# Decode key scores moved into the projection stage, and expert rows added to the residual by indirect DMA, in a hybrid decoder layer on one Trainium2 core

## What is computed

```python
h = rmsnorm(x)
sq, sk, sv, dq, dk, dv, ga, gb = split(h @ w_in)          # 3*512, 3*768, 2*1024 columns
# branch A, stick-breaking attention, 8 heads of 64, for prompt rows over the prompt,
# for the 8 decode rows over 16 pages of 128 keys each, found through page_table:
z = q @ k.T / 8 + bias
a = exp(log_sigmoid(z) + sum of log_sigmoid(-z) over the later keys);  oA = a @ v
# branch B, dilated windows (128,1), (512,4), (2048,16), joined by their denominators -> oB
x = x + (sigmoid(ga) * (oA @ w_br_a) + sigmoid(gb) * (oB @ w_br_b)) @ w_out
# experts: 8 of 64 per token, weights w, plus one shared expert
h2 = rmsnorm(x)
x = x + shared(h2) + sum over the token's 8 experts of w * (silu(h2 @ wg[e]) * (h2 @ wu[e])) @ wd[e]
```

## Time and profile before

| | us |
|---|---|
| median of 3 runs | 2694.28 (2693.86 to 2694.97) |
| profiled execution | 2692.04 |
| its span, first to last instruction | 2690.2 |
| mean granted TensorE clock | 0.919 |
| busy: PE, DVE, ACT, POOL | 2252.5, 1063.6, 649.8, 685.6 |

### The profile page before, as it was taken

The page is one execution under the profiler, slowest core; times in us unless marked ns, Lnnn a source line. Parts: engine busy times, 40 slices in busy tenths (PEclk is TensorE's granted clock), DMA queues, the critical chain, the costliest instruction groups (busy, mean ns, idle before and its releaser), DMA issues. The chain is left out here.

```text
span 2690.2 us, 35840 instructions
## 1 busy us (share of the span) xinstructions
PE 2252.5 (84%) x12724; PEld 1687.6 (63%) x12724; DVE 1063.6 (40%) x1742; ACT 649.8 (24%) x1136; POOL 685.6 (25%) x711
## 2 busy tenths in 40 slices
PE   7999996492787869999799765999999999999910
PEld 6778674481343336666454524888998888889800
DVE  3000786555999720000022521333333333333367
ACT  5322221261443420000011001232232223222300
POOL 2121331000454420000000173222222222222166
PEclk9999998695899989999899887999999999999955
DMA  6657334324777750188231245999998998989788
GB/s 202 227 169 245 133 113 160 118 87 151 218 239 237 236 194 20 31 353 342 90 117 57 68 111 199 323 321 326 323 324 314 328 317 324 326 323 326 283 331 317
DMA packets 195136, 600.13 MB, mean 223 GB/s; under 512 B 27006, under 2 KB 71503, under 8 KB 168536
## 3 DMA queue, kind: packets, MB, share of 16 engines
q1 hardware_dynamic: 139200, 462.79, 49.6%
q0 software_dynamic: 24448, 77.12, 8.1%
q10 hardware_dynamic: 31392, 59.01, 5.9%
HBM read 475.54 MB, written 167.28 MB: 239 GB/s over the span
## 5 line engine op out<-in xcount | busy, mean ns | idle before, releaser
L1996 PE MATMUL pG_e<-xT,w_e 128*128 128x160 f32 x4224 | 627.0, 302 | 2.3 <-issue 1.3
L1996 PEld LDWEIGHTS pG_e<-xT,w_e 128*128 128x128 f32 x4224 | 586.4, 197 | 29.4 <-issue 26.5
L2102 DVE TENSOR_TENSOR w_e_lo<-w_e,w_e_hi 128x2048 fp32r<-128x2048 f32 x66 | 151.3, 2292 | 323.9 <-ACT w_e_hi L2043 323.9
L1379 PE MATMUL pG<-turned,w_gates 128*128 128x344 f32 x768 | 227.7, 455 | 20.3 <-DMA w_gates<-in_w_in 20.3
L504 PE MATMUL pP<-wring,hT_hi 128*128 128x512 f32 (+2 forms) x576 | 226.9, 394 | 4.9 <-POOL wring L307 3.9
L2043 ACT ACTIVATE w_e_hi<-w_e 128x2048 fp32r<-128x2048 f32 x66 | 126.1, 1911 | 399.0 <-DMA w_e<-in_w_e_down 385.1
L505 PE MATMUL pP<-wring,hT_hi 128*128 128x512 f32 (+2 forms) x576 | 221.3, 384 | 0.0
L506 PE MATMUL pP<-wring,hT_lo 128*128 128x512 f32 (+2 forms) x576 | 221.3, 384 | 0.0
L1379 PEld LDWEIGHTS pG<-turned,w_gates 128*128 128x128 f32 x768 | 147.1, 192 | 96.7 <-issue 21.6
L2092 DVE COPY xT<-pX 128x512 f32<-128x512 f32 x132 | 90.7, 687 | 246.2 <-PE pX L1980 246.2
L1958 POOL COPY index<-slot_token 128x1 int32 (+1 forms) x66 | 39.4, 597 | 576.3 <-PE pX L1983 570.0
(11 more groups left out here) (251 smaller groups left out, 3396.1 us busy)
## 6 DMA issues: line engine op xcount, KB each, us to landing
w_e<-in_w_e_gate SPq DMA_DIRECT2D x66, 1024.0 KB, 8.8
w_e<-in_w_e_up SPq DMA_DIRECT2D x66, 1024.0 KB, 11.4
w_e<-in_w_e_down SPq DMA_DIRECT2D x66, 1024.0 KB, 6.4
y_scratch<-zero SPq DMA_DIRECT2D x5, 8704.0 KB, 56.2
y_scratch<-y_e ACTq DMA_DIRECT2D x66, 512.0 KB
turned<-in_cache_sb_kv SPq DMA_DIRECT2D x128, 256.0 KB, 3.1
vbuf<-in_cache_sb_kv SPq DMA_DIRECT2D x128, 256.0 KB, 3.1
out<-in_cache_win_kv SPq DMA_DIRECT2D x8, 4094.0 KB, 18.7
```

Source lines behind the costliest of these rows:

```text
L1379: last = pe.matmul(pG[:, i % 2, k, :NC], wg[:, f // 2 % 2, k, c, (f % 2) * P:(f % 2 + 1) * P], hT[:, c, cols], start=(c == 0), stop=(c == ...
L1996: last = pe.matmul(pG[:, k, f * BLK:(f + 1) * BLK], wv[:, c, f, :], xT[:, r, c, :], start=(c == 0), stop=(c == KC - 1))
L2102: dve.tensor_tensor(wlo[:, r, :], w[:, r, 2, :], whi[:, r, :].bitcast(F32), ALU.subtract).then_inc(wlo_ready, 1)
```

## The change

1. Keys of the decode rows. Their loads, products and reductions leave the stick-breaking stage and are put into the projection: SP starts chunk n (of 32) after the store of item n + 9, VectorE scores it in its turn n + 10. There are two key buffers instead of four, in rows of `turned` that are free then; the scores go to DRAM (`sz`, 0.5 MB) and come back at the start of stick-breaking. There each decode row's remaining steps begin one tick into its five ticks instead of five, and values are loaded without waiting for keys.
2. Expert rows. `y_scratch`, its zeros and the combining stage are gone. The table of slots also carries the pair's weight, ScalarE's copies multiply by it, and GpSimd adds the rows into x2 with two indirect transfers per block, four blocks behind its gathers. Unused slots name spare rows 1032 to 1191 of h2 and x2, which are zeroed in the output stage. A last stage copies x2 to the outputs.

Projection:

```diff
+                def load_keys(n):
+                    s, c = divmod(n, NPC)
+                    if n >= NKB:
+                        sp.wait_ge(s_prod_ready, n - NKB + 1)
+                    if c == 0:
+                        sp.dma_start(q[:, s % 2, :], sc["samp"][s:s + 1, 0:SBW].broadcast_to([P, SBW])).then_inc(q_in[s % 2], 16)
+                    for j in range(GP):
+                        pg = sp.value_load(pages[0:1, n * GP + j:n * GP + j + 1], min_val=0, max_val=n_pool - 1)
+                        sp.dma_start(kbuf[:, n % NKB, j, :], pool_kv[bass.ds(pg, 1), :, 0, :].rearrange("n p d -> (n p) d")).then_inc(k_in[n % NKB], 16)
...
+                    if 0 <= i - (C0 - 1) < NCH:
+                        load_keys(i - (C0 - 1))
+                    if i == C0 + NCH + 1:
+                        sp.wait_ge(s_score_ready, NCH)
+                        sp.dma_start(sc["sz"], turned[:, 15, :]).then_inc(sz_out, 16)
...
+                def score_keys(n):
+                    s, c = divmod(n, NPC)
...
+                    dve.wait_ge(k_in[n % NKB], 16 * GP * (n // NKB + 1))
+                    if n:
+                        dve.wait_ge(s_score_ready, n)
+                    dve.tensor_tensor(prod, kbuf[:, n % NKB], q[:, s % 2, :].unsqueeze(1).broadcast_to([P, GP, SBW]),
+                                      ALU.mult).then_inc(s_prod_ready, 1)
+                    dve.wait_ge(s_prod_ready, n + 1)
+                    dve.tensor_reduce(s_z[:, s, c * GP:(c + 1) * GP, :].rearrange("p a h -> p (a h)"),
+                                      prod.rearrange("p a (h d) -> p (a h) d", d=HD), AX_X, ALU.add).then_inc(s_score_ready, 1)
...
                     if items[i]["normed"]:
                         norm(i)
+                    if 0 <= i - C0 < NCH:
+                        score_keys(i - C0)
```

Stick-breaking (the key lines are removed, the steps renumbered):

```diff
-    LOW, LN, SOFT, SUMS, LOGIT, PROB = L, L + 1, L + 2, L + 3, L + 4, L + 5
-    VALUES = [L + 5, L + 6, L + 7, L + 8]
+    LOW, LN, SOFT, SUMS, LOGIT, PROB = 1, 2, 3, 4, 5, 6
+    VALUES = [6, 7, 8, 9]
```

Routing:

```diff
                 for t in range(NT):
                     m = rows_of(t)
+                    pool.wait_ge(pairs_ready, t + 1)
                     for k in range(TOPK):
-                        pool.indirect_dma_start(sc["table"], bass.IndirectOffsetOnAxis(ap=dest[:m, t * 8 + k:t * 8 + k + 1], axis=0),
-                                                tokid[:m, t:t + 1], None).then_inc(scattered, 16)
+                        j = t * TOPK + k
+                        pool.indirect_dma_start(sc["table"], bass.IndirectOffsetOnAxis(ap=dest[:m, j:j + 1], axis=0),
+                                                pairs[:m, j, :], None).then_inc(scattered, 16)
```

Experts, GpSimd and ScalarE:

```diff
+                def aim(it, j):
+
+                    pool.tensor_copy(target[:, j % 2, :], slot_info[:, bass.ds(it * U + j, 1), :]).then_inc(target_ready, 1)
+
+                def scatter(it, j):
+
+                    r = j % 2
+                    pool.wait_ge(target_ready, it * U + (j + 1))
+                    pool.wait_ge(y_copied, it * (2 * U) + 2 * (j + 1))
+                    if seen(it, j, 1):
+                        pool.wait_ge(y_out, it * (U * 32) + 32 * j)
+                    pool.nop(nofuse=True)
+                    pool.indirect_dma_start(sc["x2"], bass.IndirectOffsetOnAxis(ap=target[:, r, 0:1], axis=0), y[:, :], None,
+                                            compute_op=ALU.add).then_inc(y_out, 16)
+                    pool.indirect_dma_start(x2_quarters, bass.IndirectOffsetOnAxis(ap=target[:, r, 1:2], axis=0), y_tail[:, :], None,
+                                            compute_op=ALU.add).then_inc(y_out, 16)
+
+                def body(it, old):
                     for j in range(U):
...
+                        gather(it, j)
+                        if old is not None:
+                            aim(old, j)
+                            scatter(old, j)
...
                 def put(it, j):
                     act.wait_ge(y_ready, it * U + (j + 1))
+                    act.wait_ge(target_ready, it * U + (j + 1))
                     if seen(it, j, 1):
-                        act.wait_ge(y_out, it * (U * PUTS) + PUTS * j)
-                    act.activation(y[:, :], pY[:, :], ACT.Copy).then_inc(y_copied, 1)
-                    act.activation(y_tail[:, :], pQ[:, :QW], ACT.Copy).then_inc(y_copied, 1)
-                    act.wait_ge(y_copied, it * (2 * U) + 2 * (j + 1))
-                    act.dma_start(sc["y"][bass.ds(it * (U * BLK) + j * BLK, P), :], y[:, :]).then_inc(y_out, 16)
...
+                        act.wait_ge(y_out, it * (U * 32) + 32 * j)
+                    act.activation(y[:, :], pY[:, :], ACT.Copy, scale=scale[:, j % 2, 2:3]).then_inc(y_copied, 1)
+                    act.activation(y_tail[:, :], pQ[:, :QW], ACT.Copy, scale=scale[:, j % 2, 3:4]).then_inc(y_copied, 1)
```

The last stage:

```diff
+            sp.dma_start(o[0][0].rearrange("(p n) d -> p (n d)", p=P), sc["x2"][:S, :].rearrange("(p n) d -> p (n d)", p=P)).then_inc(copied, 16)
+            sp.dma_start(o[1][:, 0], sc["x2"][S:T, :]).then_inc(copied, 16)
+            sp.wait_ge(copied, 32)
```

More of the change, by code:

```diff
@@ L201, in phase_project @@
         turn_copied = sem("turn_copied")
+        pages_in = sem("s_pages_in")
+        q_in = [sem(f"s_q_in{i}") for i in range(2)]
+        k_in = [sem(f"s_k_in{i}") for i in range(NKB)]
+        s_prod_ready = sem("s_prod_ready")
+        s_score_ready = sem("s_score_ready")
+        sz_out = sem("s_sz_out")
         n_normed = [sum(x["normed"] for x in items[:i]) for i in range(NI + 1)]
@@ L293, in _ @@
                         move_windows(i // NT)
+                    if i == NT - 1:
+                        sp.wait_ge(stored[i % NSTAGE], store_value[i])
+                        for u in range(2):
+                            sp.wait_ge(ht_out[u], 16 * len(range(u, NT, 2)))
+                        sp.wait_ge(pages_in, 16)
+                    if 0 <= i - (C0 - 1) < NCH:
[3 more added lines that the diff above has]
+                        sp.dma_start(sc["sz"], turned[:, 15, :]).then_inc(sz_out, 16)
                 for slot in range(NSTAGE):
@@ L296, in _ @@
                     sp.wait_ge(stored[slot], store_value[last])
-                for i in range(2):
-                    sp.wait_ge(ht_out[i], 16 * len(range(i, NT, 2)))
+                sp.wait_ge(sz_out, 16)
                 sp.wait_ge(copies_out, 16 * NG * NS)
@@ L1433, in phase_out @@
         junk = sb("junk2", [P, D])
-        zero = sb("zero_row", [1, D])
+        zero = sb("zero_row", [BLK // 5, D])
         ss = sb("ss2", [P, NT])
@@ L1964, in _, with gather @@
-                body(0)
-                with pool.Fori(1, load_last(pool) + 1) as it:
-                    body(it)
+                def gather(it, j):
+                    r = j % 2
+                    if seen(it, j, 2):
+                        pool.wait_ge(x_psum, it * (3 * U) + 3 * (j - 1))
+                    pool.tensor_copy(index[:, r, :], slot_info[:, bass.ds(it * U + j, 1), 0:2]).then_inc(index_ready, 1)
+                    pool.wait_ge(index_ready, it * U + (j + 1))
+                    pool.nop(nofuse=True)
+                    pool.indirect_dma_start(rows[:, r, :], None, sc["h2"], bass.IndirectOffsetOnAxis(ap=index[:, r, 0:1], axis=0)).then_inc(rows_in[r], 16)
+                    pool.indirect_dma_start(tail[:, r, :], None, h2_quarters, bass.IndirectOffsetOnAxis(ap=index[:, r, 1:2], axis=0)).then_inc(rows_in[r], 16)
@@ new lines, in body @@
+                def body(it, old):
+                    for j in range(U):
+                        gather(it, j)
+                        if old is not None:
+                            aim(old, j)
+                            scatter(old, j)
+                for it in range(LAG):
+                    body(it, None)
+                last = load_last(pool)
+                with pool.Fori(LAG, last + 1) as it:
+                    body(it, it - LAG)
+                for n in range(LAG):
+                    for j in range(U):
+                        aim(last - (LAG - 1 - n), j)
+                        scatter(last - (LAG - 1 - n), j)
@@ L1968, in _ @@
+                pool.wait_ge(y_out, last * (U * 32) + U * 32)
+                pool.nop(nofuse=True)
             @block.tensor
```

262 lines of the change are left out of this document (96 added, 166 removed).

## The result

| | before | after |
|---|---|---|
| median | 2694.07 us (2692.72 to 2694.97) | 2623.80 us (2621.18 to 2627.90) |
| span of the profiled execution | 2690.2 | 2618.4 |
| ratio, 95% interval | | 0.9741 [0.9724, 0.9758] |

What follows compares the result with a forecast made beforehand. It took each stage to have its own bound: VectorE in stick-breaking and normalizing, TensorE in the experts. Terms -100 - 55 + 45 + 6 + 45 = -59 us, set on the median, gave 2635 us; its own range 2595 to 2690, overall 2565 to 2830.

Steps and rivals of the forecast that it cites:

- Combining, -100: End of program: the 120.6 us combining stage goes, two DRAM copies taken as 20 us replace it; -100 us (-105 to -92).
- So nothing more: Program's end: the last block's scatter replaces a store that also had to land first, so it adds no time.
- Stick-breaking, -55: Stick-breaking stage: 150.5 us of key work leave VectorE, TensorE is next in line; -55 us (-70 to -25).
- The signs named: Stick-breaking: some 265 us instead of 323 from first to last matmul, TensorE above 95% busy at clock 1.00.
- Projection, +45: Projection: 32 key chunks at about 5 us and four stops of some 17 us delay normalizing; +45 us (+20 to +65).
- upper bound of +65: Projection: the term's slow bound, with key chunks at 6 us.
- Gate 0: Gate stage: 44.5 MB of zero stores leave, but were hidden behind a busy TensorE; 0 us.
- routing +6: Routing: first scatter waits for VectorE's eight picks, plus two transposes and four small copies; +6 us (+3 to +10).
- Experts, +45: Expert loop: adding rows into x2 lengthens each block's transfers to 14.47 us, +0.68 on 66 blocks; +45 us.
- 2 us window of 426 GB/s: Expert loop: at this rate, seen at share 1.03, a block takes 12.0 us and the add costs nothing.
- mean of two sums of shares: Expert loop: 14.47 us per block, between 14.16 (add as twice the store) and 14.78 (twice the gather).
- rival of the single y buffer: Expert loop: copy, scatter and landing of one y tile set a 17.4 us period; +238 us, 2828 us; chance 0.27.

Runs made afterwards that it cites:

- e11: Kernel after with a third, plain indirect transfer of the y rows per block into an extra scratch, and two y buffers: 2622.75 us.
- e9: Kernel after with the two indirect transfers per block storing instead of adding (output not the reference's): 2617.71 us.
- e10: Kernel after with a third, plain indirect transfer of the y rows per block into an extra scratch, still one y buffer: 2812.59 us.
- e12: Kernel after with all eight moves of the old cache taken from the projection to the gate stage: 2573.35 us.
- e8: Kernel after with second buffers for y and its quarter rows, ScalarE waiting for the scatter two blocks back: 2626.18 us.
- e7: e3 with all keys loaded but nearly all of VectorE's arithmetic on them left out (scores not the reference's): 2580.39 us.
- e3: Kernel after with four of the eight old-cache moves put at projection items behind the key chunks: 2593.74 us.
- e6: e3 with only the first two key chunks loaded and the other 30 scored from the same buffers: 2576.60 us.

## Why the prediction came near, and where it was wrong

That 2635 us came near is luck in good part. By stages the forecast missed by +29 us (projection), -44 (experts), +6 (combining) and -5 (stick-breaking), and with a small rest these cancel to -13.

- **Combining, -100: right, a little large.** Measured -94.2. The copy took 15.4 us, not 20; but from the last expert matmul to the next stage's start it is 17 us, where it was 6 (a wait of 7.74 for the single y buffer, then two issues and a landing). "So nothing more" was the wrong step, by 11 us.
- **Stick-breaking, -55: right.** -60.5, with VectorE at half load and TensorE next, as forecast. The signs named came too: TensorE is 97% busy at a clock of 1.00 in the middle of the stage, and from first to last matmul it is 258 us, where it was 320 (265 and 323 were named). Of TensorE's 47 us of waits for GpSimd's masks 6 are left, so most of them went with VectorE's key work.
- **Projection, +45: the right mechanism, the stops rightly sized, the start and the pace between stops too small.** The four stops are there: the products before and after a stop stand 21.3 to 22.5 us apart, 87.7 in all, where 4 x (17 + 5) = 88 were counted. The start was taken as 85 us and is 102.83: the first keys were issued at 91.60, behind the item's store and the load of q, and took 11 us. And from product to product the other 27 steps are 155.5 us, 5.76 each instead of 5, and the last chunk 5.4. That is 18 and 21 us more, less 7 for a last chunk that the forecast counted once too often: 32, which is 76.6 - 45. (Behind the start of normalizing the stage is 2.3 us shorter than before, hence 74.3.) Its upper bound of +65 ("chunks at 6 us") was too near, because it kept the early start. That this half helps (-55 + 45 = -10) is wrong in sign: alone it costs 16 us.
- **Gate 0, routing +6: right** (0.3 and 7.6).
- **Experts, +45: wrong, and the step is the claim that a block's DMA time above 13.79 us becomes the period.** The period stayed (+1.4 us in all). The add's size was well taken, 3.17 us measured between the bounds of 1.68 and 5.97 and near twice the store (3.36). But `e11` holds the period with 1.03 x 13.79 = 14.2 us of engine time per block. The 2 us window of 426 GB/s, which spoke for this, deserved more than the mean of two sums of shares. `e9` has the scatter at 11.4% of the engines and the kernel after at 23.0; the rule of the Trainium skill (Collectives: The Full Stack, the bandwidth ceiling and fold count) that an adding transfer runs at half the rate of a copying one, stated there for collectives, agrees with that. `e11` moves 359 GB/s on the mean while TensorE never waits, and the adds' second read isn't in that figure, since queue 0 counts 75.67 MB with adds and 75.44 without. So the limit of about 358 GB/s in the Trainium skill (DMA: Bandwidth & Descriptors, Specifications) does not show as one here. The Trainium skill also says (DMA: Bandwidth & Descriptors, the section Measured) that each core gets about that much when both cores of the memory domain stream; this kernel runs on one core, and no run here has a second.
- **The rival of the single y buffer did not come true, but it is the right mechanism.** It was said to need a landing of 13.6 us, from three gathers. The landing is 9.5, and the round has 4.3 us beside it, not the 1.8 counted: GpSimd's first issue (1.93) and part of the hand-over weren't in it. The sum is 13.76 us, level with TensorE. 3 us more, in `e10`, and it was 189 us of the program, a landing of only 10.2 sufficing.

Still open: how the 28 us by which normalizing starts later in `e12` than in the kernel before divide. Loads and arithmetic have about 10 and 15 of it with late moves, by the two ways shown above; why GpSimd's instruction gets longer beside VectorE's work no run tells. Nor does a run tell whether the order on SP's queue or the full engines hold the keys behind a copy (share 1.04 from 110 to 127 us), since none issues the copies from another queue. With the keys loaded once VectorE still waits for the rows of q, which are loaded just ahead of their first chunk:

```profile
DVE turned L506 <- DMA turned<-samp_scratch: 28.6, 5, 10.5
```

## What to carry to other kernels

Work moved to an idle engine brings its loads along, and these stand in order on a queue: look at what is ahead of them there. Here copies of 5.4 MB, harmless as long as only stores stood behind them, cost 50 of the 60 us that the move won elsewhere, and the remedy was to move the copies, not the keys.

For a buffer that is filled, sent and filled again, add up the whole round (copy, hand-over, every issue, landing) and set it against the period. If it is within a few per cent, as here, the next small addition can cost its full length in every block, and a second buffer is the cheap insurance. A wait that appears in nearly every block is the sign, even when it costs nothing yet.

Take halves of a change apart even when the whole is faster.

## What was not expected of the hardware

- A DMA share above 1.0 held over 800 us at an unchanged period: 1.01 with 322 GB/s, 1.03 with 359.
- An indirect scatter of 0.5 MB lands after 9.8 to 9.9 us whether it stores or adds (11.2 for the add with two buffers, `e8`), while its engine time about doubles with the add, and GpSimd's issue goes from 1.02 to 1.62 us.
- The third scatter's issue took 2.2 us (median) in `e10` and 0.99 in `e11`, with the same instruction but for the buffer. In `e11` it is the gather of 128 rows whose issue is long, 2.37 us on average from 1700 to 2500, where it takes 0.98 in `e10`. Why wasn't tried.
- A GpSimd subtraction of 128 x 512 elements takes 1.30 us beside a VectorE that hardly works (`e7`, 18 of 185 us busy) and 1.68 to 1.75 beside its key products and reductions (`e3`, `e6`).
